# Where the last two modulation tiles are multiplied in a fused three-block kernel

## What is computed

```python
mod = silu(c) @ w_ada + b_ada                     # [1024] @ [1024, 6144]
sh1, sc1, gt1, sh2, sc2, gt2 = split(mod, 6)
h = rms_norm(x, g_pre_mix) * (1 + sc1) + sh1
y = hybrid_mixer(h, w_in, ..., w_out)
x = x + gt1 * rms_norm(y, g_post_mix)
h = rms_norm(x, g_pre_ffn) * (1 + sc2) + sh2
y = moe_ffn(h, w_router, b_router, w_mlp1, b_mlp1, w_mlp2, b_mlp2)
x = x + gt2 * rms_norm(y, g_post_ffn)
```

## Time and profile before

| | |
|---|---|
| device time of three runs | 2637.76 us median, 2636.64 and 2644.43 the others |
| the profiled execution | span 2643.0 us, 39144 instructions; of the three times, 2644.43 is the one above it |
| PE busy | 2496.3 us (94%) |
| DVE, ACT, POOL busy | 1329.3, 913.3, 261.3 us |
| DMA | 713.68 MB, mean 270 GB/s |
| mean granted TensorE clock | 0.979 |
| chain that ended last | PE 51%, DVE 3%, ACT 2% of the span, the rest not assigned |

### The profile page before, as it was taken

One profiled execution on the slowest core, in us unless ns is written; L12 is line 12 of the kernel. 1 busy time (PEld: TensorE's weight loads), 2 busy tenths in 40 slices (PEclk: granted clock), 3 DMA queues, 4 the chain that ended last, 5 costly groups with the idle time before them and its releaser, 6 DMA issues.

```text
span 2643.0 us, 39144 instructions
## 1 busy us (share of the span) xinstructions
PE 2496.3 (94%) x16618; PEld 1762.0 (67%) x16618; DVE 1329.3 (50%) x1846; ACT 913.3 (35%) x1243; POOL 261.3 (10%) x181
## 2 busy tenths in 40 slices
PE   7988999999989999879999999999999999999998
PEld 5652323333323333278899899998899999887997
DVE  4451222212223222188777755756665765785755
ACT  4441111111111111056555544553444444435443
POOL 3000000000000000021000101262011201202200
PEclk9999999999999999989999999999999999999999
DMA  9689999999999999953455566555466466451562
GB/s 335 212 311 425 427 428 406 427 428 427 428 423 414 427 428 428 427 182 132 152 199 192 183 207 208 178 172 191 163 223 208 159 208 207 136 171 38 177 210 103
DMA packets 248986, 713.68 MB, mean 270 GB/s; under 512 B 12563, under 2 KB 186345, under 8 KB 223910
## 3 DMA queue, kind: packets, MB, share of 16 engines
q1 hardware_dynamic: 237424, 690.26, 68.8%
q10 hardware_dynamic: 9446, 15.97, 1.8%
q0 software_dynamic: 1936, 4.87, 0.6%
HBM read 710.01 MB, written 1.05 MB: 269 GB/s over the span
## 4 chain that ended last, share of the span: by engine, by line
PE 51%; DVE 3%; ACT 2%; issue 1%; POOL 0%; DVEq 0%; ACTq 0%; POOLq 0%
PE bank L429 19%; PE bank L671 13%; PE bank L434 10%; PE bank L623 4%; PE bank L703 2%; ACT ap L3945 1%; PE bank L899 1%; PE bank L2680 1%; PE bank L3456 0%; PE bank L467 0%; DVE stats L3219 0%; DVE xa L3217 0%; PE bank L4025 0%; ACT hi L362 0%; PE bank L3759 0%
## 5 line engine op out<-in xcount | busy, mean ns | idle before, releaser
L371 DVE TENSOR_TENSOR lo<-ring,hi 128x2048 fp32r<-128x2048 f32 x251 | 601.8, 2403 | 249.1 <-ACT hi L362 248.8
L362 ACT ACTIVATE hi<-ring 128x2048 fp32r<-128x2048 f32 x251 | 476.0, 1900 | 136.3 <-PE bank L671 106.8
L2130 PE MATMUL bank<-expert,xg 128*64 128x512 f32 x1664 | 387.6, 604 | 29.0 <-DMA expert<-in_w_mlp 28.1
L429 PE MATMUL bank<-x_hi,hi 128*128 128x256 f32 (+1 forms) x1576 | 369.1, 279 | 0.0
L429 PE MATMUL bank<-x_lo,hi 128*128 128x256 f32 (+1 forms) x1576 | 366.7, 278 | 0.0
L429 PEld LDWEIGHTS bank<-x_hi,hi 128*128 128x128 f32 (+1 forms) x1576 | 296.1, 188 | 3.3 <-issue 1.8
L429 PEld LDWEIGHTS bank<-x_lo,hi 128*128 128x128 f32 (+1 forms) x1576 | 296.0, 188 | 2.2 <-issue 0.7
L2130 PEld LDWEIGHTS bank<-expert,xg 128*64 128x64 f32 x1664 | 114.0, 137 | 241.7 <-issue 208.0
L2260 DVE TENSOR_TENSOR acc<-bank,acc 128x512 f32<-128x512 f32 x100 | 62.1, 683 | 332.7 <-PE bank L2238 332.6
L434 PE MATMUL bank<-x_hi,lo 128*128 128x256 f32 (+1 forms) x1576 | 197.0, 278 | 0.9 <-DVE lo L371 0.9
L2213 PE MATMUL bank<-expert,aT 128*64 128x512 f32 x832 | 185.7, 596 | 5.5 <-DMA expert<-in_w_mlp 5.5
(11 more groups left out here) (697 smaller groups left out, 3908.5 us busy)
## 6 DMA issues: line engine op xcount, KB each, us to landing
expert<-in_w_mlp SPq DMA_DIRECT2D x192, 2048.0 KB, 18.9
ring<-in_l_ffn_w_in SPq DMA_DIRECT2D x88, 1024.0 KB, 5.1
ring<-in_l_ffn_w_out SPq DMA_DIRECT2D x44, 1024.0 KB, 4.9
ring<-in_w_ada SPq DMA_DIRECT2D x24, 1024.0 KB, 7.0
ring<-in_l_gm_w_in SPq DMA_DIRECT2D x24, 1024.0 KB, 5.2
ring<-in_ffn_w_up SPq DMA_DIRECT2D x22, 1024.0 KB, 5.1
ring<-in_w_in SPq DMA_DIRECT2D x21, 1024.0 KB, 7.4
ring<-in_l_gm_w_out SPq DMA_DIRECT2D x12, 1024.0 KB, 4.9
```

The costliest lines, as they stand in the source:

```text
L362: e.activation(k.half("hi", u), k.slot(j), ACT.Copy).then_inc(*k.up("hi_done"))
L371: e.tensor_tensor(k.half("lo", u), k.slot(k.units[u][0]), k.half("hi", u).bitcast(F32), SUB).then_inc(*k.up("lo_done"))
L429: e.matmul(o, l, r, start=fresh, stop=False, skip_group_check=True)
L2130: i = e.matmul(banks[n][j][h * CAP:(h + 1) * CAP, :], x, W[:, (2 * h + j) * 512:(2 * h + j + 1) * 512], start=c == 0, stop=False, skip_gro ...
```

## The change

All four halves of tiles 10 and 11 are multiplied in `mixer_out_pe`, right behind the output projection, and none in `route_pe`. Both copies of the rows are made in `mixer_out_act`, behind the modulated rows that ScalarE makes, and none in `route_act`. Loads, `dense_left`, flips and all else stay as they are; since the banks are released at once, the rotation hands out other banks in the routing.

```diff
@@ mixer_out_pe
     for flag in PE_:
         k.mark(flag, "meet", "post1")
-    late_ada_pe(k, e, 10, 0)
+    for i in LATE:
+        for h in range(2):
+            late_ada_pe(k, e, i, h)
     met(k, e, "post1")
     turn_rows_pe(k, e, "pre2", done=k.dve)
@@ mixer_out_act
     upper_act(k, e, "pre2", t["s2"], t["mod"][:, 24:32], t["x"], 4, "out", True)
+    for i in LATE:
+        late_row_act(k, e, i)
@@ route_pe
     to_tok_pe(k, e, "htok", t["x"])
-    late_ada_pe(k, e, 10, 1)
     bank, tri, one = k.bank(e, "places"), k.cc("tri"), t["one1"]
...
     m.then_inc(*k.MM("places"))
-    late_ada_pe(k, e, 11, 0)
     e.wait_ge(*k.act("htok", 1, 1))
...
     for n in OF[0]:
         turn_x_pe(k, e, n)
-    late_ada_pe(k, e, 11, 1)
@@ route_act
     e.activation(t["gates"], t["gates"], ACT.Exp).then_inc(*k.ACT("gates"))
-    late_row_act(k, e, 10)
     for n in OF[0]:
         select_x_act(k, e, n)
     for n in OF[0]:
         turn_x_act(k, e, n)
-    late_row_act(k, e, 11)
     e.wait_ge(*k.mm("gT"))
```

## The result

The changed kernel takes 2642.51 us (median of 12), the kernel before 2637.36 (median of 12): ratio 1.0023, interval 1.0013 to 1.0033. That is 5 to 6 us slower, where 2 us faster was forecast, and outside the range given. By the bound of 0.3% it is no change, but the interval leaves no doubt of its sign.

What follows compares the result with a forecast made beforehand. The DMA stream of expert weights was taken as the bound; load 4 earlier by 1.4 + 0.1 + 0.5 = 2.0 us starts it 2.0 us earlier, giving 2635.8 us against the median 2637.76. Range 2633.0 to 2641.0.

Steps and rivals of the forecast that it cites:

- The bound: Expert stage: the DMA engines bound some 900 us, with a DMA share of 0.96 to 1.01 from 190 to 1090 us.
- (a): TensorE behind the projection: four halves take 4.0 us in the idle time, 1.8 us are left; cost 0.
- (b): ScalarE behind the modulated rows: two copies, about 1.1 us, end 0.35 us before they would delay anything; cost 0.
- (c): SP's issues: load 3 goes out at about 169.8 instead of 183.37, off the path; gain 0.
- (g): PSUM banks: the rotation gives other banks to turned rows and logits, whose former users are finished; cost 0.
- (d): SP's issues: load 4, expert 1's first, no longer waits for tile 11; gain 1.4 us on load 4.
- (e): TensorE in the routing without the halves: load 4 gains 0.1 us, first expert product and load 5 gain 0.3.
- (f): Clock at the turned rows: the filled pause may keep it up; 0.5 us taken, ends 0 and 0.9.
- the sum: Start of the expert stream: load 4 comes 2.0 us earlier, load 5 0.8; no gap, so the stream gains 2.0.
- rival 1: Expert stream: TensorE paces it and load 5 decides, not load 4; gain 0.3 to 1.2 us, say 0.7; chance 0.2.
- rival 2: Routing: without the halves the clock falls at about 185 and load 5 comes late; 2.1 us slower; chance 0.18.
- Rival 3: Pauses hid the halves and the freed ring slots were not waited for in earnest; gain 0; chance 0.12.

Runs made afterwards that it cites:

- fill3: Changed kernel plus three groups of four matmuls, read by nobody, where the three halves stood in the routing; 0.9990 against the kernel before, 0.9977 again.
- fillA: Changed kernel plus one group of four filler matmuls, only in the pause before the mask; 0.9993 against the kernel before.
- tfill3: Changed kernel plus three groups of eight 128x128 filler transposes where the three halves stood; 0.9994 against the kernel before.
- late_loads: Changed kernel with expert load 3 also waiting for the places and load 4 for expert 0's turned selection; 1.0020 against the kernel before.
- fill5: Changed kernel with filler matmuls in the three routing pauses and two more groups behind the four halves; 1.0003 against the kernel before, 0.9984 again.
- after_again: The changed kernel measured and profiled again, nothing else changed; 1.0018 against the kernel before.
- after: The changed kernel as first measured and profiled; 2642.51 us, 1.0023 against the kernel before.
- tile11_back: Changed kernel with tile 11's two halves and its row copy put back into the routing; 1.0005 against the kernel before.
- fillBC: Changed kernel plus filler groups behind the places and behind the turn, none before the mask; 1.0003 against the kernel before.
- fill3_late_loads: Changed kernel with filler in the three routing pauses, load 3 waiting for the places, load 4 for the turned selection; 1.0000 against the kernel before.

## Why the prediction was wrong, point by point

- **The bound** was read rightly: from the expert loads to block 2 the DMA stream decides. Which load sets it was read wrongly, see below.
- **(a)** right, even a little cheap: 3.64 us for the four halves (4.0 said), 2.18 left over (1.8). **(b)** right, the copies ended 0.47 us ahead. **(c)** right: load 3 at 169.46, no effect. **(g)** no wait on a bank showed.
- **(d)** right for load 4's issue, as fill3 shows: it comes 1.48 us earlier, 0.14 of it through an earlier selection, 1.34 (1.4 said) for the wait on tile 11. In the changed kernel itself even that is used up: the order of the experts comes as much later. That it is a gain for the kernel is wrong, see the first of the two steps.
- **(e)** was worth nothing. fill3 can't test it, since filler stands where the halves stood; in fillA, with two of the three pauses empty and the clock held, load 5 is 0.09 us earlier than before, less than the 0.14 by which the selection is.
- **(f)** was mis-sized. The clock fell all the same at the turned rows, only later, and rose again at the same distance: 0.14 us at the selection, where 0.5 stood in the sum. What it would be worth held is 0.7 (0.9 was the bound).
- **The first step that failed** is in the sum: "1.6 - 1.2 = 0.4 us are left, no gap. The stream starts 2.0 us earlier". It took the queue in front of load 5 for slack that load 4 could give up. In fill3, with the clock held, load 4 is 1.48 us earlier and load 5 0.14, and the stream is ahead by the 0.14 (loads 5 to 13) and by nothing in its bytes (376 GB/s over 60 us in both); tfill3 and fillA show the same (load 4 1.49 earlier, load 13 0.18 and 0.09). So **rival 1** was right, at a chance of 0.2: load 5 sets the stream. The gain without the fall is 0.1 us at the loads, below its 0.3, since (e) gave nothing and (f) little.
- **The step that made the sign wrong** is in rival 2: "TensorE is still busy for more than half of the routing, and the pauses at 179 and 183 did not lower the clock before." I took the pauses of before, of 0.5 us each, for the pauses after. With the halves gone they are 1.45 and 1.09 us, and from 181.9 to 186.0 us TensorE works 1.6 of 4.1 us. I had the places of both (182.2 to 183.7, 185.3 to 186.4) in the text and didn't add them up. That gave this course a chance of 0.18; both profiles of the changed kernel, and late_loads, show it.
- **Its price** was too small as well, 2.1 us against 4.8. I ended the slow stretch within the first expert products and put load 5 at 199.0, 3.7 us late; the stretch lasted 13.6 us, to 198.5, and load 5 came 4.8 us late, which is 1.1 more. The other 1.6 us are again the queue, which was to hide them: it hid nothing, here or in late_loads, where load 5 is 4.7 us late and the bytes are the same 342 GB/s. (late_loads' shorter distance to block 2, 3.3 us over before, arises later in the expert stage.)
- **Rival 3** falls: the wait on tile 11 was real, 1.34 us.
- The page "TensorE: Matmul & The Clock Gate" of the Trainium skill says (Part 4: PE-mode transpose) that transposes don't count as busy in the same way. Where it says so its figures are for bf16. tfill3 does not agree: three groups of eight float32 transposes, with matmuls around them, held the clock at 1.00, and for this kernel the measurement decides. Whether they ran in the mode that the page means, the trace does not show. So I was right to doubt it here, but the rival that it spoke for came true for another reason.

fill3 is the change with its side effect mended. It beats the changed kernel (0.9990 and 0.9977 against 1.0023 and 1.0018). What the edit was for, an earlier load 4, it then gets, and it is worth nothing: before_fill, the old kernel with five groups of idle matmuls, has load 5 at the same 26.97 as fill5, which has the change too.

Two things stay open. By its second measurement fill3 is also faster than the kernel before, by 0.1 to 0.3%, and it is 9.1 us faster than after_again, measured beside it; load 5 accounts for 0.14 and 4.94 us of these. And from block 2 to the end 1490 to 1503 us pass from one profile to the next, which hides any gain of 2 us in a single span.

## What to carry to other kernels

Work that fills TensorE's pauses does two jobs, and the second shows nowhere in a list of waits: it keeps the clock. Before moving such work, add up what TensorE does in the stretch that is left behind, not pause by pause, and price a fall by everything that is late until the clock is back. If the work must go, matmuls or transposes into a bank that nobody reads can hold its place; in these runs they delayed nothing on the path.

An earlier load is worth something only if the loads behind it come earlier too. Where the next ones wait for TensorE, follow them: here the issue of load 5, and not that of load 4, told the issue of load 13 to 0.01 us. And test such a claim close to the change; a thousand microseconds later one execution differed from the next by as much as the effect.

## What was not expected of the hardware

- In the changed kernel and its variants the clock falls at nearly the same places, wherever a profile shows a fall: 7 us (6.5 to 7.4) and 17 us (16.8 to 17.4) behind the first late half. It fell while TensorE was at work again (tile11_back, 183.1), once the thin stretch was over, not in the pause.
- How long a fall lasts varies: 3.4 us (fill3, fillBC), 6.9 (tile11_back), 10 (fill3_late_loads), 13.6 (after, after_again, late_loads). In the changed kernel the clock came back at 198.5, when the first expert products, and small products between them, had run for 5.9 us almost without a pause (from 192.58).
- A half of eight 128x32 by 128x512 instructions costs 0.87 us behind others of its kind (32 in 3.64 us), though a single instruction takes about 0.6: four of them, each for its own quarter of the columns, start within 0.02 us of each other and run together.
- A lead of 1.48 us for one load of the stream was gone within 60 us (fill3 against before), because the loads behind it were no earlier.
